# Gate stage of a mixer kernel: token norm factor multiplied in at the eviction, modulation rows loaded ahead of x

## The reference, cut to what matters

```python
def rms_norm(x, g):
    y = x * rsqrt(mean(x * x, axis=-1) + EPS)
    return y * g
...
sh, sc, gt = split(silu(cond) @ w_ada[i] + b_ada[i], 3)
h = rms_norm(x, norm_g[i]) * (1.0 + sc) + sh
u, g = split(h @ w_in, 2)
out = (fourier_mix(u) * silu(g)) @ w_out
```

## Time and profile before

| | us |
|---|---|
| median of 3 runs | 2184.42 |
| the profiled execution | 2182.24 |
| its span | 2180.4 |
| gate stage in the span, last Silu starts | 262.93 |
| TensorE busy | 2118.4 (97%) |
| VectorE busy | 1353.3 (62%) |
| ScalarE busy | 890.4 (41%) |

### The profile page before, as it was taken

One profiled execution on the slowest core, in us unless ns is written; L12 is line 12 of the kernel. 1 busy time (PEld: TensorE's weight loads), 2 busy tenths in 40 slices (PEclk: granted clock), 3 DMA queues, 4 the chain that ended last, 5 costly groups with the idle time before them and its releaser, 6 DMA issues. The chain is left out here.

```text
span 2180.4 us, 32995 instructions
## 1 busy us (share of the span) xinstructions
PE 2118.4 (97%) x13347; PEld 2031.4 (93%) x13347; DVE 1353.3 (62%) x2074; ACT 890.4 (41%) x1652; POOL 1.6 (0%) x8
## 2 busy tenths in 40 slices
PE   7999999989999999999999999999999999989997
PEld 2999877989999999999999999989999999989997
DVE  4787554664158888888755322238888888875223
ACT  3521142233124333333433333346666666664120
POOL 0000000000000000000000000000000000000000
PEclk9999999999999999999999999999999999999999
DMA  8354343585234454555544544461344443208332
GB/s 340 131 188 159 126 141 134 198 318 178 71 134 167 133 164 145 149 156 150 172 161 170 215 160 160 141 243 53 147 165 165 165 160 133 90 6 274 109 130 87
DMA packets 124822, 342.69 MB, mean 157 GB/s; under 512 B 14336, under 2 KB 69760, under 8 KB 114432
## 3 DMA queue, kind: packets, MB, share of 16 engines
q1 hardware_dynamic: 124672, 340.61, 45.3%
HBM read 225.70 MB, written 114.82 MB: 156 GB/s over the span
## 5 line engine op out<-in xcount | busy, mean ns | idle before, releaser
L2072 PE MATMUL o_ps<-o_y_hi,o_w 128*128 128x384 f32 x1536 | 394.8, 337 | 12.1 <-DVE o_y_lo L2180 9.2
L2072 PEld LDWEIGHTS o_ps<-o_y_hi,o_w 128*128 128x128 f32 x1536 | 280.0, 189 | 13.6 <-DVE o_y_lo L2180 9.3
L2072 PE MATMUL o_ps<-o_y_lo,o_w 128*128 128x384 f32 x768 | 258.3, 336 | 0.0
L2488 ACT ACTIVATE a_e<-a_ps,a_nmax 128x1152 f32<-128x1152 f32 x127 | 155.5, 1224 | 62.6 <-DVE a_nmax L2556 62.6
L2445 PE MATMUL a_ps<-a_v_hi,a_at_hi 128*128 128x256 f32 x576 | 172.9, 300 | 0.0
L2556 DVE TENSOR_REDUCE a_nmax<-a_ps 128x1 f32<-128x1152 f32 x127 | 171.8, 1353 | 0.2 <-PE a_ps L2412 0.2
L2445 PE MATMUL a_ps<-a_v_lo,a_at_hi 128*128 128x256 f32 x576 | 162.5, 282 | 0.0
L2445 PE MATMUL a_ps<-a_v_hi,a_at_lo 128*128 128x256 f32 x576 | 162.1, 281 | 0.0
L2072 PEld LDWEIGHTS o_ps<-o_y_lo,o_w 128*128 128x128 f32 x768 | 145.4, 189 | 0.0
L2180 DVE TENSOR_TENSOR o_y_lo<-o_y_raw,o_y_hi 128x384 fp32r<-128x384 f32 x94 | 50.6, 555 | 128.6 <-ACT o_y_hi L2127 128.5
L968 PE MATMUL p_ps<-p_late_hi,p_w_lo 128*128 128x384 f32 x384 | 128.3, 334 | 0.0
(11 more groups left out here) (326 smaller groups left out, 5377.9 us busy)
## 6 DMA issues: line engine op xcount, KB each, us to landing
p_w_raw<-w_in_dram SPq DMA_DIRECT2D x32, 1024.0 KB, 4.8
o_y_raw<-y_dram SPq DMA_DIRECT2D x96, 192.0 KB, 3.6
g_wada<-w_ada_dram SPq DMA_DIRECT2D x16, 1024.0 KB, 6.8
f_w_raw<-w_u_dram SPq DMA_DIRECT2D x32, 512.0 KB, 4.3
o_w_raw<-w_out_dram SPq DMA_DIRECT2D x32, 512.0 KB, 4.2
g_dram<-g_stage SPq DMA_DIRECT2D x16, 576.0 KB, 3.2
f_g<-g_dram SPq DMA_DIRECT2D x8, 1152.0 KB, 7.6
y_dram<-f_y SPq DMA_DIRECT2D x8, 1152.0 KB, 5.3
```

The costliest lines, as they stand in the source:

```text
L2072: mm = pe.matmul(ps[:, d, 0:CH], a, m, start=(e == 0 and j == 0), stop=(e == ET - 1 and j == 2))
L2488: act.activation(split3(e[:, m % 2, half, :]), ps[:, 3 * half:3 * half + 3, 0:CH], ACT.Exp, bias=nmax[:, m % 2, half:half + 1], scale=1.0, ...
```

## The change

The products now work on x times the scale alone: `h_hi` and `h_lo` are the parts of scale times x. The token factor is constant along the channels, so VectorE multiplies it in when it evicts a half from PSUM to `stage` (`scale`). The shift is no longer added to x ahead of the products: its two columns (latent, context) stand as columns 1152 and 1153 of `h_hi` and `h_lo`, and their product comes out as two more columns of the third bank, `lift`, which Silu adds as its bias. Silu now reads `stage` in two pieces. The banks are free when the half is scaled, no longer when Silu is done. SyncE loads all w_ada rows ahead of x; the sums of squares and the spreading of the token factor come in the middle and at the end of unit 0's products. The token factor stays in `sh.ss` for the whole stage, and the norm of x itself (which the Fourier stage needs) moves from unit 0 to rounds 1 to 3 (NORMS), followed by ScalarE's shift. The w_ada rows for the later modulation go in 32 halves of 1024 columns through three buffers.

```diff
--- before.py
+++ after.py
@@ tiles and banks
-        sq = at("sq", [P, 2, T], 65536)
+        sq = at("sq", [P, 2, T], 189376)
-        h_hi = at("h_hi", [P, DT, T], 0, F32R)
-        wada = at("wada", [P, 2, 2 * D], 36992)
+        h_hi = at("h_hi", [P, DT, T + 2], 0, F32R)
+        wada = at("wada", [P, 3, D], 36928)
-        first = sh.ss[:, 0:2 * 514].rearrange("p (a b) -> p a b", b=514)
+        first = at("first", [P, 2, 514], 49280)
+        lift = at("lift", [P, 2, 2], 149664)
-        TURNED, LAM, SUMS, SPREAD = 4, 5, 7, (5, 6, 7)
+        TURNED, LAM, SUMS, SPREAD = 4, 5, 3, (7, 3, 7)
-        HALF_ROWS = [(), (0, 1, 2), (3, 4, 5), (6, 7), (8, 9), (10, 11, 12), (13, 14, 15), ()]
+        PIECES = [(slice(0, NS), 0), (slice(NS, T), 1)]
+        NORMS = [(), (0, 1, 2), (3, 4, 5), (6, 7), (), (), (), ()]
+        HALF_ROWS = [range(a, b) for a, b in ((0, 0), (0, 6), (6, 12), (12, 16), (16, 20), (20, 26), (26, 32), (32, 32))]
@@ sync
             sp.dma_start(wada0[:, 0, :], w_ada[0, 0][:, 0:2 * D]).then_inc(wada0_in[0], 16)
-            sp.dma_start(x[:, 0, 0:T], x_in[0]).then_inc(x_tile_in[0], 16)
...
             for k in range(1, DT):
                 sp.dma_start(wada0[:, k, :], w_ada[0, k][:, 0:2 * D]).then_inc(wada0_in[k], 16)
+            sp.dma_start(w_raw[:, 0, :], w_src[0]).then_inc(raw_in[0], 16)
+            for k in range(DT):
                 sp.dma_start(x[:, k, 0:T], x_in[k]).then_inc(x_tile_in[k], 16)
-            for s in range(2):
-                sp.dma_start(w_raw[:, s, :], w_src[s]).then_inc(raw_in[s], 16)
+            sp.dma_start(w_raw[:, 1, :], w_src[1]).then_inc(raw_in[1], 16)
...
+                sp.dma_start(wada[:, r % 3, :], w_ada[layer, row][:, third * D:(third + 1) * D]).then_inc(wada_in[r % 3], 16)
...
-                    if r + 2 < 2 * DT:
+                    if r + 3 < 4 * DT:
                         sp.wait_ge(weighed_done, r + 1)
-                        load_wada(r + 2)
+                        load_wada(r + 3)
@@ tensor
-                return pe.matmul(ps[:, 4 * b + c, 0:CH], a, xv[:, c * CH:(c + 1) * CH],
+                return pe.matmul(ps[:, 4 * b + c, 0:CH + 2 if c == NCH - 1 else CH], a, xv[:, wide(c)],
                                  start=(d == 0 and j == 0), stop=(d == DT - 1 and j == 2))
...
-            pe.wait_ge(rms_done, NCH)
-            pe.wait_ge(row_out, NQ)
-            pe.wait_ge(mod_ready, 1)
             pe.wait_ge(lo_ready[0], 1)
-            for k, (c, d) in enumerate(STEPS):
-                pe.wait_ge(h_lo_done, k + 1)
+            pe.wait_ge(shift_split, 2)
+            pe.wait_ge(lam_exp, 1)
+            for d in range(DT):
+                pe.wait_ge(h_lo_done, d + 1)
                 for b in range(2):
                     for j, (a, xv) in enumerate(operands(0, b, d)):
-                        mm = product(0, b, d, j, c, a, xv)
+                        for c in range(NCH):
+                            mm = product(0, b, d, j, c, a, xv)
...
+                if d == 4:
+                    square_sums()
+                if d == 6:
+                    spread(0)
+                    spread(1)
+            spread(2)
             for n in range(1, H):
                 s = n % 2
                 pe.wait_ge(lo_ready[s], n // 2 + 1)
                 for b in range(2):
-                    pe.wait_ge(drained[b], n)
+                    pe.wait_ge(scaled[b], n)
@@ scalar
             split_hi(0)
+            for k in range(3):
+                square(k)
+            act.wait_ge(mod_mm, 1)
+            for q in (1, 3):
+                act.copy(rows[:, q * BANK:(q + 1) * BANK], ps[0:2, q, :]).then_inc(row_out[1], 1)
+            act.wait_ge(mod_ready, 1)
+            for d in range(DT):
+                act.wait_ge(x_tile_in[d], 16)
+                for tok, m in PIECES:
+                    op = act.activation(h_hi[:, d, tok], x[:, d, tok], ACT.Identity, scale=sh.mod[:, 0, DT + d, m:m + 1])
+                op.then_inc(h_hi_done, 1)
+                if d == 0:
+                    act.copy(h_hi[:, :, T:T + 2], sh.mod[:, 0, 0:DT, :]).then_inc(shift_split, 1)
+                if d + 3 < DT:
+                    square(d + 3)
+            split_hi(1)
...
             for n in range(H):
                 if 1 <= n < H - 1:
                     split_hi(n + 1)
...
+                for d in NORMS[n - 1] if n > 0 else ():
+                    act.wait_ge(t_done, d + 1)
+                    for tok, m in PIECES:
+                        op = act.activation(x[:, d, tok], x[:, d, tok], ACT.Identity, bias=sh.mod[:, 0, d, m:m + 1])
+                    op.then_inc(shifted, 1)
                 for b in range(2):
...
-                    act.activation(split3(stage[:, b, :]), banks(b), ACT.Silu).then_inc(drained[b], 1)
+                    act.wait_ge(scaled[b], n + 1)
+                    for tok, m in PIECES:
+                        op = act.activation(stage[:, b, tok], stage[:, b, tok], ACT.Silu, bias=lift[:, b, m:m + 1])
+                    op.then_inc(drained[b], 1)
@@ vector
+            def scale(n, b):
+                dve.wait_ge(proj_done, 2 * n + b + 1)
+                if n > 0:
+                    dve.wait_ge(stored[b], 16 * n)
+                dve.tensor_tensor(split3(stage[:, b, :]), banks(b), split3(sh.ss[:, :]), ALU.mult)
+                dve.tensor_copy(lift[:, b, :], ps[:, 4 * b + NCH - 1, CH:CH + 2]).then_inc(scaled[b], 1)
...
+            scale(0, 0)
+            scale(0, 1)
...
                 if n in SUM_UNITS:
                     for k in range(PER):
                         add_up(PER * SUM_UNITS.index(n) + k)
+                for d in NORMS[n]:
+                    norm(d)
                 for r in HALF_ROWS[n]:
                     weigh(r)
...
+                scale(n, 0)
                 for d in FOLDS[n]:
                     fold_tile(d)
+                scale(n, 1)
```

More of the change, by code:

```diff
@@ L343, in modulated_gate @@
         mod_mm = sem("mod_mm")
-        row_out = sem("row_out")
+        row_out = [sem(f"row_out{k}") for k in range(2)]
+        shift_split = sem("shift_split")
+        scaled = [sem(f"scaled{s}") for s in range(2)]
         mod_turned = sem("mod_turned")
@@ L364, in modulated_gate @@
         stored = fold.stored
-        wada_in = [sem(f"wada_in{s}") for s in range(2)]
+        wada_in = [sem(f"wada_in{s}") for s in range(3)]
         weighed_done = sem("weighed_done")
@@ L447, in _, with square_sums, spread @@
                     pe.matmul(ps[:, LAM, 0:2], sh.ones[:, :], lam2[:, :], start=True, stop=True).then_inc(lam_mm, 1)
[L449 to L453, removed]
             for j in range(2 * DT):
                 if j * P % BANK == 0:
-                    pe.wait_ge(row_out, j * P // BANK + 1)
+                    q = j * P // BANK
+                    pe.wait_ge(row_out[q % 2], q // 2 + 1)
                 mm = pe.transpose(ps[:, TURNED, 2 * j:2 * j + 2], rows[:, j * P:(j + 1) * P], sh.ident[0:2, 0:2])
             mm.then_inc(mod_turned, 1)
[L459 to L465, removed]
+            def square_sums():
+                pe.wait_ge(ss_step, DT)
+                for t in range(TT):
+                    mm = pe.matmul(ps[:, SUMS, t:t + 1], sh.ss[:, t * P:(t + 1) * P], sh.ones[:, 0:1],
+                                   start=(t == 0), stop=True, skip_group_check=True)
+                mm.then_inc(rms_summed, 1)
+            def spread(c):
+                if c == 0:
+                    pe.wait_ge(rms_inverted, 1)
+                if c == 2:
+                    pe.wait_ge(rms_done, 1)
+                for m in range(NCH):
+                    t = NCH * c + m
+                    mm = pe.transpose(ps[:, SPREAD[c], m * P:(m + 1) * P], sh.rms[:, t:t + 1].to_broadcast([P, P]), sh.ident[:, :])
+                mm.then_inc(rms_spread, 1)
             def turn_sums(group):
                 if group % PER == 0:
-                    pe.wait_ge(weighed_done, DT * (group // PER) + DT)
+                    pe.wait_ge(weighed_done, 2 * DT * (group // PER) + 2 * DT)
                 if group >= 2:
@@ L513, in _, with square @@
             act.activation(sh.cond[:], cnd[:], ACT.Silu).then_inc(silu_done, 1)
-            for k in range(DT):
+            def square(k):
                 act.wait_ge(x_tile_in[k], 16)
@@ L562, in _, with add_square @@
             dve.tensor_scalar(sh.subln[:, :], sh.subln[:, :], 1.0 - LAM_INIT, None, ALU.mult).then_inc(subln_done, 1)
-            for k in range(DT):
+            def add_square(k):
                 dve.wait_ge(sq_done, k + 1)
@@ L569, in _ @@
                     dve.tensor_tensor(sh.ss[:, :], sh.ss[:, :], sq[:, k % 2, :], ALU.add).then_inc(ss_step, 1)
-            dve.wait_ge(mod_mm, 1)
-            for q in range(NQ):
-                dve.tensor_copy(rows[:, q * BANK:(q + 1) * BANK], ps[0:2, q, :]).then_inc(row_out, 1)
             def split_lo(n):
@@ L580, in _ @@
             split_lo(0)
-            dve.wait_ge(rms_rooted, 1)
```

(6 more changed lines are left out.)

113 lines of the change are left out of this document (49 added, 64 removed).

## The result

The kernel after takes 2202.57 us, the median of 4 runs (2198.83 to 2204.34); the kernel before took 2185.51 (2183.34 to 2186.91) beside it. The ratio is 1.0077, 95% interval 1.0059 to 1.0094: slower, by 17 us. The forecast was 2201, in a range of 2194 to 2208. The profiled execution of after took 2203.37 us, its span is 2201.5.

What follows compares the result with a forecast made beforehand. TensorE, 97% busy, was taken as the bound. Terms of -2.8, +0.3, +2.0, +12.5, +0.4 and +1.7 us made +14.1, half clock +2.4 made +16.5; on 2184.4 this gave 2201, range 2194 to 2208.

Steps and rivals of the forecast that it cites:

- Part 1, the head: Start of the gate stage: w_ada rows loaded ahead of x bring the first product to 42.0, 6.6 us earlier.
- Part 2, unit 0: First unit's products: TensorE becomes the bound; half pace and a new wait leave unit 1 at 75.1, 2.8 us gained.
- Part 3, the eviction: Scaling from PSUM takes 1.36 us, Silu in two pieces 1.42; two extra columns cost at most 0.4 us in all.
- Part 4, round 1: VectorE's pass serving unit 1: 25.7 us against 25.3, with 0.6 for a load; 0.3 lost, unit 2 at 100.7.
- rival (b): In the w_ada half rows, loads take 5 to 6 us: the sum becomes +19 to +25, 2204 to 2210; 10%.
- Rounds 2 and 3: VectorE's passes serving units 2 and 3: TensorE waits 2.0 us before unit 3, 12.9 for unit 4's first sum.
- The rest: From the restart in unit 4 to the next stage: half clock +2.4, units 5 to 7 lose 0.5, tail +1.7.
- Rival (a): VectorE's load stays covered in the gate stage: only head and tail count, -1.1 us, 2183, or 2181 at full clock; 7%.
- rival (d): The gate stage's head gets no shorter, the modulation being no earlier: 6.6 us more, 2207.5; 4%.
- Rival (c): Half clock also follows the short waits ahead of units 1 and 3, costing 1.6 us: 2202.5 or 2204; 30%.

Runs made afterwards that it cites:

- both orders: The changed kernel with split_hi of unit n+2 between unit n's Silus, and fold 3 and unit 5's split_lo behind awaited sums: 2185.26 us, ratio 1.0004.

## Why the prediction was right

The sign, the place and the size held: 17.1 us against 16.5, by the mechanism that was forecast. A part of the closeness is luck, as errors of single steps cancel: against the forecast, after is 0.6 us late at the first product, 1.6 at unit 2, and only 0.7 at the restart, the first sum of unit 4 (172.53 for 171.8). Step by step:

- **Part 1, the head.** First product at 42.62, forecast 42.0. The 0.6 lies in the first three rows of w_ada: they end at 19.2, where 6.93 and the two prices give 18.6. These 24 matmuls took 11.8 to 13.3 us in the profiles of the kernels with all w_ada rows ahead of x, so this is within what one execution differs from another. From the last modulation product to the finished modulation 2.5 us were forecast and 2.46 measured (36.84 to 39.30), and no use waited for x.
- **Part 2, unit 0.** 33.24 us (42.62 to 75.86) against 33.1. The half clock came as carried over (granted clock 0.90; the first 18 products took 5.77 us where three take 0.53 at full clock, 2.6 more for a forecast of 2.4), the wait was 2.12 for 2.4. The kernels with the early spread and with the added matmuls show each of these two terms separately. Two slips of the working each leave the sum a few tenths short: 0.90 over the 28.4 us of the earlier trace rows makes 5.7 us at 1.2 GHz, not 5.3, and the wait named as 2.4 stands in the sum as 2.2.
- **Part 3, the eviction.** The group of 16 scalings has a mean of 1.346 us, the squares added from SBUF one of 1.353:

```profile
L647 DVE TENSOR_TENSOR g_stage<-g_ps,ss 128x1152 f32<-128x1152 f32 x16 | 21.5, 1346 | 17.6 <-ACT ss L571 10.6 <-PE g_ps L492 7.0
...
L598 DVE TENSOR_TENSOR ss<-ss,g_sq 128x1152 f32<-128x1152 f32 x7 | 9.5, 1353 | 0.2
```

  So 1.36 held, and the 0.06 more for a PSUM source that the Trainium skill gives (VectorE: DVE Perf Modes, the section on the TRN2 errata) is not there. Silu in two pieces took 1.44 for 1.42. The extra columns cost nothing.
- **Part 4, round 1.** The one term that was sized clearly wrong: the load wait was 1.43 us, not 0.6. So unit 2 started 26.41 us after unit 1, for 25.6; this and the 0.8 by which unit 1 was late put it at 102.27 instead of 100.7. The wait comes behind the two short halves of row 0 and one full half, near where I looked for it; its length was read from the median landing time of 4.2 us, and a median says nothing of one load. This one was issued at 88.38 and had landed at 93.50, 5.1 us later; the twelve loads of rounds 1 and 2 took 3.4 to 5.1. This is a part of rival (b), which is otherwise refuted: the other such waits of the gate stage add up to 0.3 us.

```profile
93.50 7.26 DVE L671 SCALAR_TENSOR_TENSOR g_weighed<-g_wada,cond_silu,g_weighed 128x1024 f32<-128x1024 f32 x6 [1.43 <-DMA g_wada<-w_ada_dram]
```

- **Rounds 2 and 3.** 26.99 us for 27.3, with a wait of 1.38 us ahead of unit 3 for 2.0, and from unit 3 to the restart 43.27 for 43.8. The wait was 11.99 us, forecast 12.9: VectorE was at the sum 0.7 us later than forecast, TensorE asked for it 1.6 us later.
- **The rest.** From the restart in unit 4 to the next stage 112.28 us, against 107.68 before: 4.6 more. Forecast were 2.4 (half clock), 0.5 (units 5 to 7; the sum has 0.4) and 1.7 (tail), 4.6. The tail by itself is 1.7 by TensorE's idle time, 6.62 against 4.91.
- **Rival (a)**, the load covered, and **rival (d)**, no shorter head, are refuted by the first sum at 172 and the first product at 42.6. The rule of the Trainium skill that stood beside (a) (Perfetto Trace Analysis, section Identifying the Most-Contended Engine), to optimize the most occupied engine first, names TensorE, and TensorE's time did decide. But it decided by a wait of 11.99 us for VectorE, 62% busy, and not by TensorE's own work, so occupancy alone did not tell which way this change goes. **Rival (c)**, half clock behind the short waits, is not in after's profile, but it is in others of this study (below).

What the forecast did not see is how little of the loss belongs to the change. The queue of VectorE was taken as given; the kernel with both orders shows that the same work fits with no wait in units 2 to 7. What the change puts ahead of the first sum (the norms, the scalings and the fold between them) moved VectorE past the point at which the old order breaks, which was 0.4 us away before. How much each of these parts weighs was not separated; no kernel has the new eviction without the moved norms.

## What to carry to other kernels

When an eviction moves to an engine that already has a hand-made order, the order is part of the change: write its queue out up to the first result that TensorE wants, and move what nobody waits for behind it. Look for the chain, not the load: here VectorE was idle for 3.3 us, waiting for ScalarE, in the very stretch in which TensorE waited 12 us for VectorE. An early start at a stage's head is worth what the rest of the stage keeps of it: of 6.0 us, 2.1 were left at unit 1, and the wait, the half clock and the tail behind the last product each had to be recovered on its own. Even then the fastest kernel is only 0.2% below the kernel before (ratio 0.9982, 0.9973 to 0.9991).

## What was not expected of the hardware

- **A wait of 2.1 us sometimes costs the clock and sometimes not.** With both orders, the row at 75.94 shows three products in 1.30 us behind a wait of 2.12; in after's profile the row at 75.86 has 0.77 behind the same wait. The kernel without the shift's columns has both a 2.06 and a 1.84 wait followed by slow products, in the rows shown with it. In the four kernels in which the wait was 0.51 or 0.52 no slow row stood there. What decides between the cases was not found.
- **Full clock came with work that nobody reads**: 1.00 in place of 0.90 to 0.92 over unit 0.
- **Single executions differ by more than small edits.** After's own runs span 5.5 us. Up to the next stage its profile is 17.1 us behind before's, at the end of the span 21.1, though nothing behind the gate stage was changed. Two places with a lower clock are part of this: the granted clock is 0.89 over 1465 to 1480 and over 1966 to 1981, and 1.00 in the stretches of before that lie 17 and 21 us earlier. The medians differ by 17.1. The other 4 us come from which executions were profiled: after's lies 0.8 us above its median, before's (2182.24) 3.3 below the 2185.51 that stands beside it.
